# A 20-stage transformer kernel: the memory's key and value products moved to other places of the program

## The reference

```
mem_n = rmsnorm(mem, norm_mem)
for i in range(4):
    hn = rmsnorm(x, norm_mix[i])
    mix = diff_attention | hgrn2 | chunked_sgu | diff_attention   # by i
    x = x + mix
    x = x + mem_cross_attention(rmsnorm(x, norm_cross[i]), mem_n, ca_w_q[i], ca_w_kv[i], ca_w_o[i])
    x = x + swiglu(rmsnorm(x, norm_ffn[i]), ffn_w_gu[i], ffn_w_down[i])
return rmsnorm(x, norm_final)

def mem_cross_attention(h, mem_n, w_q, w_kv, w_o):   # 4 heads of 256
    q = h @ w_q;  k, v = split(mem_n @ w_kv)
    p = softmax(q k^T / 16);  return (p v) @ w_o
```

## Time and profile before

| | before |
|---|---|
| median of 3 runs | 3304.18 us (3299.82 to 3309.08) |
| the profiled execution | 3312.77 us, of which the trace's span is 3311.0 us |
| TensorE busy | 3090.5 us, 93% of the span |
| GpSimd, ScalarE, VectorE busy | 2125.7, 1310.5, 1219.5 us |
| mean granted TensorE clock | 0.956 of full |

### The profile page before, as it was taken

How to read it: one execution, slowest core, us unless ns; L and a number is a source line. 1 busy time by engine, 2 the same in 40 slices (tenths; PEclk the granted TensorE clock), 3 DMA queues, 4 the chain that set the end, 5 groups by cost and what they waited for, 6 DMA issues and landing times.

```text
span 3311.0 us, 56431 instructions
## 1 busy us (share of the span) xinstructions
PE 3090.5 (93%) x24448; PEld 3008.9 (91%) x24448; DVE 1219.5 (37%) x1933; ACT 1310.5 (40%) x1335; POOL 2125.7 (64%) x464
## 2 busy tenths in 40 slices
PE   7999899999998999869999978999999999879998
PEld 7999789999997999859899977989999899769998
DVE  3226443132364331553331286243132421542421
ACT  3344434343444433423343542443344333333432
POOL 6876458877764678535587750748758487627585
PEclk9999899999998999979999989999999999979999
DMA  6544335554442455413355420535445355414353
GB/s 217 184 173 152 116 132 179 186 178 179 174 152 102 149 181 181 167 62 133 123 179 178 179 89 1 179 116 186 171 152 179 115 185 183 142 61 168 125 182 115
DMA packets 73442, 496.87 MB, mean 150 GB/s; under 512 B 8027, under 2 KB 12763, under 8 KB 14084
## 3 DMA queue, kind: packets, MB, share of 16 engines
q1 hardware_dynamic: 67768, 485.85, 41.1%
q10 hardware_dynamic: 5452, 7.62, 0.9%
HBM read 490.01 MB, written 3.41 MB: 149 GB/s over the span
## 4 chain that ended last, share of the span: by engine, by line
PE 81%; DVE 10%; issue 3%; DMA 2%; ACT 2%; POOL 2%; DVEq 0%; SPq 0%; POOLq 0%
PE G L402 20%; PE G L403 19%; PE G L404 19%; PE S L403 5%; PE S L404 5%; PE S L402 5%; DMA raw<-w_units 2%; PE G L609 2%; POOL wl L363 2%; DVE al L1412 1%; PE S L825 1%; DVE pt L1622 1%; DVE small L1574 1%; ACT wh L932 1%; DVE prob L1604 1%
## 5 line engine op out<-in xcount | busy, mean ns | idle before, releaser
L363 POOL TENSOR_TENSOR wl<-raw,wh 128x2048 fp32r<-128x2048 f32 x460 | 2125.5, 4630 | 1154.2 <-ACT wh L932 1139.2
L932 ACT ACTIVATE wh<-raw 128x2048 fp32r<-128x2048 f32 x456 | 870.3, 1912 | 1187.8 <-DMA raw<-w_units 1187.7
L402 PE MATMUL G<-ah,wl 128*128 128x256 f32 x4368 | 1255.3, 287 | 25.9 <-DVE hv L1479 10.5
L403 PE MATMUL G<-al,wh 128*128 128x256 f32 x4368 | 1247.9, 286 | 0.0
L404 PE MATMUL G<-ah,wh 128*128 128x256 f32 x4368 | 1246.9, 285 | 0.0
L402 PEld LDWEIGHTS G<-ah,wl 128*128 128x128 f32 x4368 | 851.2, 195 | 39.9 <-issue 23.8
L403 PEld LDWEIGHTS G<-al,wh 128*128 128x128 f32 x4368 | 851.7, 195 | 0.1
L404 PEld LDWEIGHTS G<-ah,wh 128*128 128x128 f32 x4368 | 850.6, 195 | 0.0
L403 PE MATMUL S<-gl,wh 128*128 128x256 f32 x1408 | 398.5, 283 | 0.0
L404 PE MATMUL S<-gh,wh 128*128 128x256 f32 x1408 | 397.8, 282 | 0.0
L402 PE MATMUL S<-gh,wl 128*128 128x256 f32 x1408 | 394.6, 280 | 0.0
(11 more groups left out here) (339 smaller groups left out, 4075.3 us busy)
## 6 DMA issues: line engine op xcount, KB each, us to landing
raw<-w_units SPq DMA_DIRECT2D x460, 1024.0 KB, 4.8
bias<-tables ACTq DMA_DIRECT2D x24, 128.0 KB, 4.5
...
```

Source lines behind the costliest of these rows:

```text
L363: pool.tensor_tensor(wl[:, j * UW:(j + 1) * UW], raw[:, j * UW:(j + 1) * UW], wh[:, j * UW:(j + 1) * UW].bitcast(F32), ALU.subtract)\
L402: pe.matmul(out, sl, vh, start=start and k == 0, stop=False, **kw)
L403: pe.matmul(out, sh, vl, start=False, stop=False, **kw)
L932: act.activation(wh[:, j * UW:(j + 1) * UW], raw[:, j * UW:(j + 1) * UW], ACT.Copy)\
```

## The change

The 32 units of the memory's keys and values keep their number and their matmuls; only their places and the engine that copies them change.

- **Keys** (4 units a layer) move out of `cross` into the mixer ahead of it. In diff they go after groups 5 and 6 and in the two places of `head_norm` where `keep_warm` stood. The other units of diff are spread anew: three instead of two ahead of the attention, one after each of the groups 0 to 4; the wait for the next pair's keys moves from behind the units to the head of `score`. In hgrn the keys stand between the second and the third run of four units. In sgu they replace the two `keep_warm(24)` (48 rows each in the trace), two units each.
- **Values** (4 units a layer): one in `cross` behind the queries, three between the scores and the first group's transposes, followed by a wait for their copies. The queries come first in `cross` and start from `ah`, `al`.
- Keys and values get tiles of their own, `kc` and `vc`, and ScalarE copies them out of G (`copy_memory`), behind the weight cut of the same step. It signals with a new semaphore, `mem_copied`.
- **The memory's norm** moves into the last feed-forward stage of the first block: load, squares, root, scaling and cuts between its units.

The core of the diff:

```diff
+    ex_at = at[0] - 4 * 4096
+    kc, vc = sb("kc", 2048, offset=ex_at), sb("vc", 2048, offset=ex_at + 4 * 2048)
+    memx, memn = sb("memx", 2048, offset=ex_at), sb("memn", 2048, offset=ex_at + 4 * 2048)
...
+                    if memory and u == 13:
+                        norm_sums(memn)
+                        c.next(acts_ready, KD // 2)
...
-                if i == 0:
-                    norm_sums()
-                    c.next(acts_ready, KD // 2)
-                projection(2, copied, ah, al)
+                projection(3, copied, ah, al)
...
+                if keys:
+                    projection(1, mem_copied, mh, ml)
+                else:
+                    keep_warm(WARM["head_norm"])
                 pe.wait_ge(vec_to_pe, c.next(vec_to_pe))
...
+                    if g and qb == 0:
+                        pe.wait_ge(vec_to_pe, c.next(vec_to_pe))
...
                 def between(g):
 
-                    if g % 2 == 0 and g < 6:
-                        projection(2, copied, ah, al)
-                        pe.wait_ge(vec_to_pe, c.next(vec_to_pe))
+                    if g < 5:
+                        projection(1, copied, ah, al)
+                    elif g < 7:
+                        projection(1, mem_copied, mh, ml)
 
                 attention(groups_diff(), score, values, prob2, pt2, between)
-                head_norm(prob2, WARM["head_norm"])
+                head_norm(prob2)
                 projection(4, x_ready, oh, ol, acts_ready)
...
                 row_sums()
                 projection(2, copied, ah, al)
                 projection(4, act_out, ah, al)
+                projection(4, mem_copied, mh, ml)
                 projection(4, copied, ah, al, kind="tokens")
                 projection(4, act_out, ah, al)
 
...
                 row_sums()
                 projection(2, act_out, ah, al, kind="tokens")
                 projection(4, act_out, ah, al)
-                keep_warm(WARM["gating"])
+                projection(2, mem_copied, mh, ml)
                 pe.wait_ge(vec_to_pe, c.next(vec_to_pe))
                 for n in range(2):
...
             def cross(i):
-                projection(2, copied, mh, ml)
+                projection(2, copied, ah, al, acts_ready)
                 row_sums()
-                projection(2, copied, mh, ml)
-                projection(4, copied, mh, ml, kind="tokens")
-                projection(4, copied, ah, al, acts_ready)
+                projection(2, copied, ah, al)
+                projection(1, mem_copied, mh, ml, kind="tokens")
                 pe.wait_ge(vec_to_pe, c.next(vec_to_pe))
+                pe.wait_ge(mem_copied, expect[mem_copied.name] - 1)
+
+                def between(g):
+                    if g == 0:
+                        projection(3, mem_copied, mh, ml, kind="tokens")
+                        pe.wait_ge(mem_copied, expect[mem_copied.name])
 
                 def score(g, out):
...
+            def copy_memory(n, u, values=False):
+
+                act.wait_ge(unit_done, n + 1)
+                bank = g_next()
+                if values:
+                    to = vc[:, :].rearrange("p (b n) -> p b n", b=2)[:, :, u * 256:(u + 1) * 256]
+                    ins = act.activation(to, bank[:, :].rearrange("p (b n) -> p b n", b=2), ACT.Copy)
+                else:
+                    ins = act.activation(kc[:, u * 512:(u + 1) * 512], bank[:, :], ACT.Copy)
+                ins.then_inc(mem_copied, c.one(mem_copied))
+
+            def memory_unit(u, values=False):
+
+                step()
+                copy_memory(unit[0] - 1, u, values)
...
+                    if memory and u == 8:
+                        act.wait_ge(memory_in, 16)
+                        for k in range(KD // 2):
+                            act.activation(memn[:, k * 512:(k + 1) * 512], memx[:, k * 512:(k + 1) * 512],
+                                           ACT.Square).then_inc(squares_ready, c.one(squares_ready))
+                    if memory and u == 12:
+                        square_root(1, 1.0 / D)
+                    if memory and u == 16:
+                        cut(mh, (0, 1), memn)
+                    if memory and u == 18:
+                        cut(mh, (2, 3), memn)
...
-                passed(4)
-                if i == 0:
-                    act.wait_ge(memory_in, 16)
-                    act.wait_ge(vec_to_act, c.next(vec_to_act))
-                    norm(memx, mh, updated=False)
-                passed(2)
+                passed(7)
                 sbank[0] += 1
                 act.wait_ge(vec_to_act, c.next(vec_to_act))
                 act.activation(small[:, 18:20], small[:, 18:20], ACT.Exp)\
                     .then_inc(act_to_vec, c.one(act_to_vec))
-                exps(groups_diff(), prob2, 1.0,
-                     between=lambda g: passed(2 if g % 2 == 0 and g < 6 else 0))
+
+                def between(g):
+                    if g < 5:
+                        passed(1)
+                    elif g < 7:
+                        memory_unit(g - 5)
+
+                exps(groups_diff(), prob2, 1.0, between=between)
                 act.wait_ge(vec_to_act, c.next(vec_to_act))
                 for k in range(2):
                     act.activation(prob2[:, k * 1024:(k + 1) * 1024], full[:, k * 1024:(k + 1) * 1024],
                                    ACT.Square).then_inc(squares_ready, 1)
                 inverse_root(1, 1.0 / P, rows=KD)
+                memory_unit(2)
                 sbank[0] += 2
+                step()
                 inputs_read[0] = unit[0]
                 cut(oh)
+                copy_memory(unit[0] - 1, 3)
                 out_units()
...
             def cross(i):
                 cut_input(f"norm_cross{i}")
-                passed(2)
                 input_root()
-                passed(2 + 4 + 4)
+                passed(4)
                 inputs_read[0] = unit[0]
-                exps([dict(s, outs=2) for s in groups_cross()], prob2, 1.0 / 16)
+                memory_unit(0, True)
+
+                def between(g):
+                    if g == 0:
+                        for u in range(1, 4):
+                            memory_unit(u, True)
+
+                exps([dict(s, outs=2) for s in groups_cross()], prob2, 1.0 / 16, between=between)
...
                 act.activation(he[:, :], he[:, :], ACT.Exp, scale=-1.0).then_inc(act_step, c.one(act_step))
                 act.wait_ge(*c.latest())
                 act.activation(he[:, :], he[:, :], ACT.Ln, bias=1.0).then_inc(act_to_vec, c.one(act_to_vec))
+                for u in range(4):
+                    memory_unit(u)
                 passed(4)
 
                 act.wait_ge(vec_to_act, c.next(vec_to_act))
...
+                memory_unit(0)
+                memory_unit(1)
                 sbank[0] += 2
+                step(2)
                 inputs_read[0] = unit[0]
                 cut(soh)
+                copy_memory(unit[0] - 2, 2)
+                copy_memory(unit[0] - 1, 3)
                 out_units()
 
             def send_tables():
...
+            def scale_memory():
+
+                bank = s_next()[:, 0:T]
+                r = root[:, 0:T]
+                dve.wait_ge(root_ready, c.next(root_ready))
...
+                for q in range(KD):
+                    s = full_ready if q % 2 else vec_step
+                    dve.scalar_tensor_tensor(memn[:, q * T:(q + 1) * T], memx[:, q * T:(q + 1) * T],
+                                             pcol("norm_mem", q), bank, ALU.mult, ALU.mult).then_inc(s, c.one(s))
+                dve.wait_ge(*c.latest())
+                dve.memset(flag, 0.0).then_inc(mean_used, c.one(mean_used))
...
+                    if memory and p == 7:
+                        scale_memory()
+                    if memory and p == 9:
+                        lows(memn, mh, ml)
...
                 def between(g):
                     if g % 2 == 0 and g < 6:
                         pair = (g // 2 + 1) * 512
-                        copy_units(1, qf[:, pair:pair + 512])
                         copy_units(1, kf[:, pair:pair + 512])
                         dve.wait_ge(*c.latest())
                         dve.memset(flag, 0.0).then_inc(vec_to_pe, c.one(vec_to_pe))
+                    elif g < 4:
+                        pair = (g // 2 + 2) * 512
+                        copy_units(1, qf[:, pair:pair + 512])
+                    elif g < 7:
+                        passed(1)
...
             def cross(i):
                 cut_input(f"norm_cross{i}")
-                copy_units(2, kf, memory=True)
                 input_root()
-                copy_units(2, kf[:, 1024:2048], memory=True)
-                copy_units(4, vt, tokens=True, memory=True)
                 copy_units(4, qf)
+                passed(1)
                 dve.wait_ge(*c.latest())
                 dve.memset(flag, 0.0).then_inc(vec_to_pe, c.one(vec_to_pe))
...
+        kv = columns_of(v["ca_w_kv_2"][i])
```

(8 more changed lines are left out.)

70 lines of the change are left out of this document (41 added, 29 removed).

## The result

The changed kernel takes 3222.6 us (median of 4 runs, 3218.8 to 3230.0), the kernel before beside it 3306.0 (4 runs, 3299.8 to 3309.1). The ratio is 0.9748, with a 95% interval of 0.9731 to 0.9765: 83 us faster. The forecast was 3225. The profiled execution took 3229.98 us, of which the span is 3228.2. TensorE is busy for 94% of it, at a mean granted clock of 0.968 (0.956 before).

What follows compares the result with a forecast made beforehand. TensorE, busy 93% of the span, was taken to bound the kernel, with only time between units to gain. Terms summed to 80.2 us off the profiled 3312.77 (3232.6), 3224 from the median; forecast 3225 us, range 3190 to 3262.

Steps and rivals of the forecast that it cites:

- The likeliest case: Whole kernel: the forecast itself, 3225 us with 3203 to 3247 as its own range; chance 0.55.
- Units ahead: Diff's units ahead of the attention, layer 0: the memory's norm leaves, -9.3 us; in a feed-forward stage it costs +3.5.
- Diff's attention: Diff, layers 0 and 3: nine units cover the groups' waits, 102 us each, -30.6 and -26.2 us.
- 9 units afterwards: 51.9: Diff's attention: five of its own units and four of keys take 51.9 us.
- The wait of 6.5: Sgu, ahead of the output units: the last unit covers 5.8 of 12.3 us, leaving 6.5 of wait.
- ScalarE's order is what gives the idle time back: Hgrn: ScalarE's second chain, behind four cuts, starts 21.2 us later; of 23.1 moved in, 1.9 are gained.
- rival 1: Diff, sgu, cross, hgrn: the stops hardly hurt and the clock stays up; 31 us less, 3193; chance 0.13.
- rival 2: Diff, cross, hgrn, sgu: clock and lock take more; 29 us more, 3253; chance 0.20.
- rival 3: Diff's groups: VectorE is the bound, so diff gains only its idle matmuls; gain 38 us, 3266; chance 0.06.
- rival 5: Whole kernel: the change does nothing, the wait moves from one place to the next; chance 0.02.
- rival 4: The 32 moved units: late ScalarE weight cuts make each find its weights late; 109 us, 3333, slower; chance 0.04.
- The signs that I gave for the stops: Diff's attention: VectorE's L1600 or L1604 stretched in most groups, up to 4.6 us.

Runs made afterwards that it cites:

- scalar_order: Changed kernel with ScalarE's output cut ahead of the weight cuts in diff and sgu, and cross's last copy ahead of its weight cut: 3227.0 us, ratio 0.9760.
- best_whole: Changed kernel with hgrn's second chain moved ahead, diff's output cut ahead of its weight cut, sgu's between the two weight cuts: 3215.3 us, ratio 0.9732.
- values_ahead: Changed kernel with all four value units ahead of the scores in the cross stages, none behind them: 3230.5 us, ratio 0.9768.
- spread_only: Kernel before with only diff's own units spread: three ahead of the attention, one behind each of groups 0 to 4: 3284.3 us, ratio 0.9934.
- warm_waits: Kernel before with 15 idle matmuls in each of diff's groups without a unit, no work moved: 3288.7 us, ratio 0.9945.
- pool_halves: Changed kernel with each GpSimd weight subtraction as two instructions of half the width: 3224.3 us, ratio 0.9745.

## Why the prediction was right, and where it was not

| Place | forecast | measured |
|---|---|---|
| feed-forward stage with the norm | +3.5 | +3.5 |
| diff, layer 0, norm and attention | -39.9 | -37.3 |
| diff, layer 3 | -26.2 | -21.3 |
| hgrn | -3.7 | -2.9 |
| sgu | -5.5 | -6.8 |
| four cross stages | -8.4 | -8.6 |
| stages with no change | 0 | -5.8 |
| sum | -80.2 | -79.2 |

Measured is the mean of two profiles of each kernel; the timed medians differ by 83.4. The likeliest case held, and so did its mechanism, but the total is closer than its terms, which is luck: 7.5 us too much for diff stand against 5.8 that I did not foresee.

- *Units ahead.* 43.51 us with seven units against 47.07 with six is -9.3, to the tenth. The norm costs its stage 3.5.
- *Diff's attention* was forecast at 102 us in both layers and took 105.2 and 108.1, then 107.4 and 103.5: 4 too little on average. Outside the units that is 54.1 us where I took 50; the 47.7 that I gave for full clock was further off. The waits were nearly right: 1.34 to 1.69 for groups 1 to 4 (0.9 to 1.5 said), 6.7 and 5.8 for group 0 (5.6 said). The mis-sized term is "9 units afterwards: 51.9". I let the clock act on the short matmuls alone. In layer 0 the unit behind group 0 took 7.9 us and the last one 7.4 where the others took 6.0, 3.3 us more; in layer 3 they took 7.2 and 7.7, and in the second profile the last one took 8.5 in both layers. The head norm's first sums (L629 here, L620 before) took 6.24, over the 5.1 that I had as their most. In layer 3 the last group waited 5.5 us for its probabilities, where layer 0 and both layers of the second profile have 1.2: VectorE's two L1698 took 5.20 there under a GpSimd instruction. The waits for `kc`, 0.6 and 0.7, were not in the sum. The end's wait, forecast at 2.8, was 1.1 and 0.
- *sgu.* The wait of 6.5 was 6.65, for the reason given: scalar_order took it away by ScalarE's order alone. The 2 us of half clock behind it came too (the output units took 28.2, behind best_whole's shorter wait of 1.66 they took 26.1). L873, ahead of it, ran at full clock, 3.7 instead of the 5.5 I had: hence -6.8.
- *hgrn.* Outside the units 21.9 us pass up to the first level where 26.4 did, the `hv` wait among them, 4.5 less; over the whole stage it is 2.9. Of the 21.9, TensorE is idle for 12.1, not the 13 to 18 that I gave as a sign; the rest is `keep_warm`. "ScalarE's order is what gives the idle time back" is right in part: the chain starts 20.9 us later, counted from the stage's start (21.2 said), but moving it ahead brought the first level only 2.8 us forward where I expected 10. What comes last then are ScalarE's copies of `full` between its weight cuts, and VectorE under GpSimd.
- *Cross.* Right in size, -2.1 a stage (-1.8 over 20 cross stages each of kernels with the code of before and of after). The three units cover only 1.4 us of wait, for which the copy's comes. values_ahead, 2.5 us a stage longer, shows their worth as waits: without them the copy's wait stands ahead of the scores and the other two are back. The values themselves took 5.4 us on average in the eight stages of the kernel before, 4.6 in the 20 and 4.5 in values_ahead, so what the clock brought there, 0.8, does not hang on where the three stand.
- *The rivals.* The stops and the clock cost about what was said: the result lies 30 us from rival 1 and from rival 2, though diff's attention alone, with its 54.1, is nearer to rival 2's 56.5 than to my 50. VectorE as the bound (rival 3) is refuted by spread_only, and rival 5 by the result. The cuts of rival 4 starve nobody: waits for `wl` are 4.7 us, 6.4 before, all in the first feed-forward stage. That the clock alone brings the gain, which was not among the rivals, is refuted by warm_waits.
- *The skill's rule on the lock* (the Trainium skill, "SBUF — State Buffer", "Who interferes with whom") holds: whoever comes second waits for the whole instruction. pool_halves shows it most plainly, as halving GpSimd's instruction cut stops of 2.84 and 3.58 us to 0.64 and 1.49. Without cover it would have cost up to 83 us by my estimate. No run takes the stops away altogether; with them halved diff's attention was 1 to 7 us shorter and the whole time the same, so the units beside them take most of it, as far as these runs tell. The signs that I gave for the stops came, with one name wrong: in layer 0 six of them stand in the attention, 2.2 to 4.7 us each, but four at the scaling of the next group's maxima (L1668).
